# A two-block model layer on one core: query norm moved into the softmax of the cross attention, its heads staggered, and three stretches of work put in another order

## What is computed

```python
# block one
y = concatenate([y_lru, y_ml, y_mo])              # y_mo: 6 heads of block attention
x = x + y @ w_out                                 # "wout": 2048 x 2048
hx = rms_norm(x, xa_norm_g)
hm = rms_norm(mem, mem_norm_g)
x = x + memory_cross_attention(hx, hm, xa_wq, xa_wkv, xa_wo)

def rms_norm(x, g):
    return x * rsqrt(mean(x * x, axis=-1) + eps) * g

def memory_cross_attention(h, mem_n, wq, wkv, wo):   # 4 heads of 128, 256 memory rows
    q = h @ wq
    k, v = split(mem_n @ wkv, 2)
    p = softmax(q @ k.T * 128 ** -0.5)
    return (p @ v) @ wo
```

## Time and profile before

| what | us |
|---|---|
| median of 3 runs | 3553.71 (3549.59 to 3554.19) |
| the profiled execution | 3552.99, its span 3550.9 |
| PE busy | 3402.8 (96%) |
| POOL, ACT, DVE busy | 1386.5, 1069.4, 898.8 |
| granted PE clock, mean of the run | 0.984 of full speed |

### The profile page before, as it was taken

One profiled execution on the slowest core, in us unless ns is written; L12 is line 12 of the kernel. 1 busy time (PEld: TensorE's weight loads), 2 busy tenths in 40 slices (PEclk: granted clock), 3 DMA queues, 4 the chain that ended last, 5 costly groups with the idle time before them and its releaser, 6 DMA issues.

```text
span 3550.9 us, 41542 instructions
## 1 busy us (share of the span) xinstructions
PE 3402.8 (96%) x15611; PEld 2766.7 (78%) x15611; DVE 898.8 (25%) x1498; ACT 1069.4 (30%) x1577; POOL 1386.5 (39%) x601
## 2 busy tenths in 40 slices
PE   6899999999988799999999999999999999999998
PEld 5877878787877477778887877887888887888786
DVE  4275423112124712310022122121111124200213
ACT  5344222223224433422222222223222222222322
POOL 3644333333442333434433333333444444444342
PEclk9999999999999899999999999999999999999998
DMA  6623222232431332233333322332333333333432
GB/s 191 195 61 95 66 77 64 79 83 77 121 109 42 102 87 79 79 85 99 97 83 83 83 78 76 83 83 78 95 96 99 95 98 92 95 99 97 139 95 71
DMA packets 604017, 329.14 MB, mean 93 GB/s; under 512 B 16620, under 2 KB 592372, under 8 KB 602884
## 3 DMA queue, kind: packets, MB, share of 16 engines
q1 hardware_dynamic: 595828, 317.57, 32.0%
q10 hardware_dynamic: 8080, 10.03, 0.9%
HBM read 314.71 MB, written 12.85 MB: 92 GB/s over the span
## 4 chain that ended last, share of the span: by engine, by line
PE 85%; issue 7%; DVE 4%; POOL 2%; ACT 2%; DVEq 0%; ACTq 0%; POOLq 0%
PE proj L614 75%; POOL w_lo L594 2%; PE s L889 2%; PE s L878 1%; PE t L655 1%; PE proj L641 1%; PE s L752 0%; DVE w_st L2531 0%; PE s L1170 0%; DVE ht_lo L1985 0%; DVE xy L2683 0%; DVE xy L2682 0%; DVE xy L2346 0%; PE s L1031 0%; PE s L614 0%
## 5 line engine op out<-in xcount | busy, mean ns | idle before, releaser
L594 POOL TENSOR_TENSOR w_lo<-raw,w_hi 128x1024 fp32r<-128x1024 f32 x572 | 1384.4, 2434 | 2112.5 <-ACT w_hi L1200 2091.7
L614 PE MATMUL proj<-ht_hi,w_hi 128*128 128x512 f32 (+1 forms) x4000 | 1557.2, 389 | 13.3 <-DVE ht_lo L2294 7.0
L614 PE MATMUL proj<-ht_hi,w_lo 128*128 128x512 f32 (+1 forms) x4000 | 1533.2, 383 | 0.0
L614 PE MATMUL proj<-ht_lo,w_hi 128*128 128x512 f32 (+1 forms) x4000 | 1532.6, 383 | 0.0
L614 PEld LDWEIGHTS proj<-ht_hi,w_hi 128*128 128x128 f32 x4000 | 754.4, 189 | 172.5 <-issue 19.7
L614 PEld LDWEIGHTS proj<-ht_lo,w_hi 128*128 128x128 f32 x4000 | 754.7, 189 | 149.9 <-issue 7.0
L614 PEld LDWEIGHTS proj<-ht_hi,w_lo 128*128 128x128 f32 x4000 | 753.9, 188 | 148.8
L1200 ACT ACTIVATE w_hi<-raw 128x1024 fp32r<-128x1024 f32 x570 | 584.2, 1054 | 773.6 <-PE proj L614 732.3
L614 PE MATMUL proj<-yh,w_hi 128*128 128x512 f32 x384 | 150.5, 392 | 3.9 <-DVE yl L2325 2.2
L614 PE MATMUL proj<-yl,w_hi 128*128 128x512 f32 x384 | 150.1, 391 | 0.0
L614 PE MATMUL proj<-yh,w_lo 128*128 128x512 f32 x384 | 150.0, 391 | 0.0
(11 more groups left out here) (473 smaller groups left out, 2321.7 us busy)
## 6 DMA issues: line engine op xcount, KB each, us to landing
raw<-in_w_in_dram SPq DMA_DIRECT2D x404, 512.0 KB, 3.8
raw<-in_w_out_dram SPq DMA_DIRECT2D x64, 512.0 KB, 4.0
raw<-in_xa_wkv_dram SPq DMA_DIRECT2D x16, 512.0 KB, 4.3
raw<-in_w_mem_kv_dram SPq DMA_DIRECT2D x16, 512.0 KB, 4.5
raw<-in_w_br_gla_dram SPq DMA_DIRECT2D x16, 512.0 KB, 3.9
raw<-in_w_br_pool_dram SPq DMA_DIRECT2D x16, 512.0 KB, 3.9
mem_tok<-in_mem_dram SPq DMA_DIRECT2D x4, 1024.0 KB, 8.0
x_tok<-in_x_dram SPq DMA_DIRECT2D x1, 4096.0 KB, 15.3
```

Source lines behind the costliest of these rows:

```text
L594: pool.tensor_tensor(w_lo[:, slot, :], raw[:, slot, :], w_hi[:, slot, :].bitcast(F32), ALU.subtract).then_inc(lo_done, 1)
L614: ins = pe.matmul(dst, w, x[:, kt, c0:c1], start=first and n == 0 and m == 0, stop=last and n == len(kts) - 1 and m == 2)
```

## The change

- **Query norm.** The tiles of x go into the query projection unnormed, scaled by the gain only: ACT's `ht_hi` (`x1_highs`) and DVE's `ht_lo` (`x1_lows`) take `xy` times `xa_norm_g`. The per-token norm `x_r` is one 128x4 column per token tile (`token_sums`, four small matmuls), and goes into the maxima and the exponentials of the softmax as a scale for each row. The tile-wide root, reciprocal and multiplications are gone (1 ACT, 17 DVE instructions), as is the copy to `n_t0`.
- **Heads staggered.** Unit 0 of "xq" runs alone, then unit 1, scores of head 0, unit 2, values of head 0, scores of head 1, unit 3, and so on; head h walks its token tiles from tile h on, and its products go to S[h], so that the next scores need wait only with their last tile.
- **Projection partials.** The first two output tiles of "xwo" are built up kt by kt between the heads (`xwo_part`).
- **Block one's order.** In the first unit of "wout" the last head's values come behind kt 10 in place of kt 7, `out_t` behind kt 14 in place of kt 12, and ACT and DVE make tiles 0 to 14 ahead of the head's work.
- **GLA's last head.** ACT makes `g_kkt` ahead of the gate's tanh.

```diff
+XA_ORDER = [[(h + x) % NT for x in range(NT)] for h in range(XA_HEADS)]
...
+            accumulate(b, 1, proj[0][:], range(8, 11), 0, ht_hi, ht_lo, (0, T), False, False, f, part=True)
             moba_values(MO_HEADS - 1)
-            accumulate(b, 1, proj[0][:], range(8, 13), 0, ht_hi, ht_lo, (0, T), False, False, f, part=True)
+            accumulate(b, 1, proj[0][:], range(11, 15), 3, ht_hi, ht_lo, (0, T), False, False, f, part=True)
             out_t(MO_HEADS - 1, a_o)
-            accumulate(b, 1, proj[0][:], range(13, 16), 5, ht_hi, ht_lo, (0, T), False, True, f)
+            accumulate(b, 1, proj[0][:], range(15, 16), 7, ht_hi, ht_lo, (0, T), False, True, f)
...
+            def token_sums(count, acc, dst):
+                pe.wait_ge(norm_acc, count)
+                for t in range(NT):
+                    ins = pe.matmul(dst[:, 4 * t:4 * t + 4], acc[:, t * P:(t + 1) * P], ones[:, 0:4], start=True, stop=True)
+                ins.then_inc(norm_sum, 1)
...
+            def xa_scores(h):
+                n = A_XA + h
+                taken(qb, h)
+                for t in XA_ORDER[h]:
+                    if t == XA_ORDER[h][-1]:
+                        pe.wait_ge(att_ok, n + 1)
+                    pe.matmul(S[t][:, 0:M], b_q[:, t * P:(t + 1) * P], k1[:, h, :], start=True, stop=True).then_inc(att_s, 1)
...
+                for x, t in enumerate(order):
+                    pe.wait_ge(att_e, n * 4 + x + 1)
+                    if x >= 2:
+                        pe.wait_ge(att_c, n * 4 + x - 1)
+                    transposes(TB[x % 2], [b_l[:, (2 * t + blk) * P:(2 * t + blk + 1) * P] for blk in range(2)]
+                               ).then_inc(att_p, 1)
+                    if x:
+                        product(x - 1)
+                product(NT - 1).then_inc(att_o, 1)
...
+            unit(b, 0, qb, 0, fresh=HT_X1)
+            token_sums(Z_X1 + KT, n_acc, TB[1])
+            unit(b, 2, qb, 1)
+            pe.wait_ge(att_y, MO_HEADS + 1)
+            xa_scores(0)
+            unit(b, 4, qb, 2)
+            xa_values(0)
+            xa_scores(1)
+            unit(b, 6, qb, 3, among=lambda: out_t(A_XA, b_o))
+            pe.wait_ge(yh_ready, YH_XA + 1)
+            xa_values(1)
+            xa_scores(2)
+            out_t(A_XA + 1, b_o)
+            xwo_part(0)
+            pe.wait_ge(yh_ready, YH_XA + 2)
+            xa_values(2)
+            xa_scores(3)
+            out_t(A_XA + 2, b_o)
+            xwo_part(1)
+            pe.wait_ge(yh_ready, YH_XA + 3)
+            xa_values(3)
+            xwo_part(2)
+            out_t(A_XA + 3, b_o)
+            xwo_part(3)
...
             act.wait_ge(att_y, MO_HEADS)
             for k in range(KT):
-                if k == 8:
+                if k == KT - 1:
                     copies(n, a_pt, CAUSAL)
                     ahead(H4["wout"], 0)
-                if k == KT - 1:
                     act.wait_ge(att_y, MO_HEADS + 1)
                 act.activation(ht_hi[:, k, :], xy[:, k, :], ACT.Copy).then_inc(norm_hi, 1)
...
+            ahead(i + H4["wout"], 2)
+            act.wait_ge(bank_free[1], i + Q2["wout"] + 1)
+            x1_highs(range(6))
+            ahead(H4["xq"], 0)
+            squares(xy[:, KT - 1, :], n_sq[:], Z_X1 + KT - 1)
+            x1_highs(range(6, KT))
             nt = {"rstd": n_rstd, "t": [n_t0, n_t1]}
-            root(2)
-            ahead(H4["xq"], 0)
-            highs(4 * H4["xq"], KT)
...
+                    act.wait_ge(att_l, (A_XA + h) * 4 + x + 1)
+                    act.activation(b_l[:, t * M:(t + 1) * M], S[t][:, 0:M], ACT.Exp, bias=b_st[:, t:t + 1],
+                                   scale=x_r[:, t:t + 1], accum_out=b_st[:, 4 + t:5 + t]).then_inc(att_e, 1)
...
+            xa_query(0)
+            ahead(H4["xq"], 2)
+            act.wait_ge(norm_sum, 2)
+            act.activation(x_r, TB[1][:, 0:16].rearrange("p (t c) -> p t c", c=4)[:, :, 0], ACT.Sqrt, scale=1.0 / D,
+                           bias=eps_rms).then_inc(norm_root, 1)
+            xa_query(1)
+            ahead(H4["xq"], 4)
+            xa_exps(0)
+            xa_copies(0)
+            xa_query(2)
+            ahead(H4["xq"], 6)
+            xa_exps(1)
+            xa_high(0)
+            xa_copies(1)
...
+                if last:
+                    gla_kkt(i)
                 unit_in(b, 9)
                 act.activation(g_z[:, 0, :], proj[0][:], ACT.Tanh, scale=0.5).then_inc(gla_act.sem, 1)
                 ahead(b, 10)
-                gla_kkt(i)
+                if not last:
+                    gla_kkt(i)
...
-            lows(xy, HT_Y, None, range(8))
+            lows(xy, HT_Y, None, range(KT - 1))
             out_tokens(MO_HEADS - 1, a_st, a_o)
-            lows(xy, HT_Y, None, range(8, KT - 2))
             moba_y(MO_HEADS - 1)
-            lows(xy, HT_Y, None, range(KT - 2, KT))
+            lows(xy, HT_Y, None, range(KT - 1, KT))
...
+            x1_tile(i + H4["wout"], i, 0)
+            x1_sum(KT - 2)
+            x1_tile(i + H4["wout"], i, 1)
+            x1_lows(range(8))
+            x1_sum(KT - 1)
+            x1_lows(range(8, KT))
+            dve.wait_ge(norm_root, 2)
+            link(dve.reciprocal(x_r, x_r))
...
+                    link(dve.tensor_reduce(b_st[:, t:t + 1], S[t][:, 0:M], AX, MAX, negate=True))
+                    dve.tensor_tensor(b_st[:, t:t + 1], b_st[:, t:t + 1], x_r[:, t:t + 1], MUL).then_inc(att_l, 1)
...
+            xa_logits(0)
+            xa_out(0)
+            xa_logits(1)
+            xa_low(0)
+            xa_out(1)
```

More of the change, by code:

```diff
@@ new lines, in xwo_part @@
+            def xwo_part(kt):
+                for q in range(2):
+                    if kt == 0:
+                        bank_wait(Q2["xwo"], q)
+                    accumulate(wb, 0, proj[q][:], [kt], q + 2 * kt, o_hi, o_lo, (0, T), kt == 0, kt == 3,
+                               (yh_ready, YH_XA), part=kt < 3, done=q == 1)
+            unit(b, 0, qb, 0, fresh=HT_X1)
+            token_sums(Z_X1 + KT, n_acc, TB[1])
+            unit(b, 2, qb, 1)
+            pe.wait_ge(att_y, MO_HEADS + 1)
@@ L981, in xwo @@
+            xa_values(3)
+            xwo_part(2)
+            out_t(A_XA + 3, b_o)
+            xwo_part(3)
+            def xwo(b, qb, first):
+                for q in range(first, 8):
                     bank_wait(qb, q)
                     accumulate(b, q // 2, proj[q % 2][:], range(4), q % 2, o_hi, o_lo, (0, T), True, True,
-                               (yh_ready, YH_XA) if fresh and q == 0 else None, done=q % 2 == 1, step=2)
-            xwo(H4["xwo"], Q2["xwo"], True)
-            xwo(H4["xwo"] + 1, Q2["xwo"] + 4, False)
+                               None, done=q % 2 == 1, step=2)
@@ L987, in _ @@
+            xwo(H4["xwo"], Q2["xwo"], 2)
+            xwo(H4["xwo"] + 1, Q2["xwo"] + 4, 0)
             norm_sums(Z_X2 + 2 * KT, n_acc)
```

153 lines of the change are left out of this document (90 added, 63 removed).

## The result

The changed kernel takes 3534.30 us (median of 5 runs, 3533.81 to 3535.78), the kernel before 3553.71 in the same series (5 runs, 3549.58 to 3556.52). The ratio is 0.9945, its 95% interval 0.9934 to 0.9957. The profiled execution has a span of 3532.0 us against 3550.9, at a granted clock of 0.987 against 0.984. The prediction said 3535.5, and 3528.5 to 3544.

What follows compares the result with a forecast made beforehand. PE was taken as the bound, holding 85% of the chain that ended last. Terms 4.6 + 6.0 + 2.9 + 4.7 = 18.2 us off the profiled 3552.99 gave 3534.8, or 3535.5 from the median; range 3528.5 to 3544.

Steps and rivals of the forecast that it cites:

- Block one: First "wout" unit: reordering lets kt 15 start at 879.2, not 884.67; gain 4.6 us (3.8 to 5.5).
- I take the middle: Block one: 4.6 taken from a gain of 5.5, since a clock fall, left open, would take 1.6.
- The norm: From "wout" to unit 1 of "xq": unit 1 done at 1079.1, not 1085.0; gain 6.0 us (5 to 7).
- a second fall: Unit 0 of "xq": ends at 1067.3, or 1068.6 if the clock falls again; 1067.7 taken.
- The heads: Staggered cross-attention heads: 55.7 us to the last `o_lo`, not 59.5; gain 2.9 us (0.5 to 3.8).
- finds its chain unchanged: Behind the last `o_lo`: DVE sets the pace in "xwo" as before, so only the end of that `o_lo` counts.
- GLA: GLA's last head: no wait for `g_kkt`, states at full clock; gain 4.7 us (4.4 to 4.9).
- The clock falls at each new wait and stays low over the values: Rival, heads: values at half clock cost 6.8 us, not 0.8; gain 12, 3541.5 us; chance 0.13.
- the row on which I set the rule aside: Heads: a 3.12 us idle without a fall, taken over the skill's transpose rule; sum 18, not about 12.
- Norm and heads give nothing: Rival: the last `o_lo` hangs on DVE and ACT; only block one and GLA gain, 9.3, 3544.4 us; chance 0.07.
- the change doesn't do what it says: Rival: the waits come back at the next meeting of engines; within 7 us; chance 0.03.
- slower: Rival: PE's clock stays at 1.2 GHz from 1051 on, through "xq" and "xwo" matmuls; 3578 us; chance 0.03.

Runs made afterwards that it cites:

- shifted: The changed kernel with two memsets of 0.485 us put in on DVE where PE waits for it, ahead of block one; 3539.25 us.
- weights_after_copies: The changed kernel with all 16 high copies on ACT ahead of squares and weight copies, and all 16 low copies first on DVE; 3531.02 us.
- block_one_undone: The changed kernel with block one's old order of kt, values and `out_t` put back on PE, ACT and DVE; 3542.12 us.
- no_fill: The changed kernel with heads still staggered, but all partial products of "xwo" behind the last head; 3539.11 us.
- the control: The changed kernel run again with no edit; 3533.37 us, ratio 0.9936 to the kernel before.
- fills_later: The changed kernel with values earlier in block one, copies ahead of weights in the norm, high copies ahead of exponentials, and "xwo" parts one place later; 3525.71 us.

## Why the prediction was right, step by step

- **Block one**, 4.6 (3.8 to 5.5): measured 5.4 in A, 5.6 when undone. The working gave 5.5, the step "I take the middle" took 0.9 off for a fall that didn't come; in shifted it came, and cost 1.4. No row gave a reason for either case; of the profiled executions with this order only that one lost the clock there, so the 5.5 would have been the better number. Kt 15 was put at 879.2 and stands at 879.50, its idle time at 2.2 and is 2.26.
- **The norm**, 6.0 (5 to 7): measured 5.1. DVE's copies were right: the last ends 17.6 behind the last matmul of "wout", as forecast (1066 less 1048.45). The mis-sized term is the pace of unit 0 behind them. I had one wait of 2 us for kt 7; there are two of 1.8, since tile 6 also comes late behind ACT's weight halves, but kt 7 hangs on its own tile, so the wait at kt 6 costs nothing more. What costs is the clock: I had split the difference between 1067.3 and 1068.6 for a second fall, and it fell behind kt 7's wait. So unit 0 ends 19.8 behind the last matmul of "wout", not 19.3. The first restart kept its clock, which was not foreseen and gained nothing, for PE then waited at kt 6. The token sums take 0.8 and not 0.5; unit 1 takes 11.0 and not 10.9. weights_after_copies shows where the waits come from: 5.0 of B go with them.
- **The heads**, 2.9 (0.5 to 3.8): from scores(0) to the end of the last `o_lo` it takes 55.9 (1130.82 less 1074.91; forecast 55.7). The waits were forecast as 2.4 and 2.4 and are 2.31 and 1.54. The chain in front of them was another than the forecast one: the product behind each maximum makes DVE's step 0.53 and not 0.65, so that DVE no longer sets the pace, but ACT's four exponentials with a scale for each row take 0.54 each, and in the first wait the query's copy (0.60), which the sum left out, stands ahead of them. The two errors nearly cancel in the first wait. No fall came here, so the gain is 3.6, less 0.4 that "xwo" starts later (banks side by side), which "finds its chain unchanged" denied. What the number hid is that it is 4.8 less 1.6. In three other profiled executions with the same code the clock fell behind the first wait; with that fall C is 1.8 to 2.3 us shorter than before, and not 3.2.
- **GLA**, 4.7: 4.64 in the stretch from the norm sums to the head's output product (345.23 to 340.59), 4.84 when undone.
- **The rivals.** "The clock falls at each new wait and stays low over the values" did not happen in the changed kernel, but it does happen: behind 2.32 to 2.34 us in block_one_undone and shifted, and behind 3.71 and 2.93 in no_fill. It costs 1.3 at 2.3 us of waiting (10.47 from the end of one wait to the next in shifted, 9.19 in the control), not the 3.4 I had priced. So the row on which I set the rule aside (3.12 us and no fall) was one sample: behind 3.31 the same products ran at half speed, in both kernels with heads in sequence. The rule of the Trainium skill, "TensorE: Matmul & The Clock Gate", section "Part 4: PE-mode transpose", that transposes don't bring the full clock, doesn't describe this mixed work either: behind 1118.68 in shifted only transposes and small products run, 6 and 8 of them, and at 1122.09 they are back at full length (0.38 for two transposes). No run here has transposes alone. "Norm and heads give nothing", "the change doesn't do what it says" and "slower" are out by the table.
- The terms' errors, +0.8, -0.9, +0.3 and 0, and 0.6 in code that nobody touched, nearly cancel. That the total was only 1.2 off is partly luck; the sizes of the single terms are good to about 1 us.

## What to carry to other kernels

- Read a change by stretches between fixed events, not by the median. Here unedited stretches moved by up to 3.3 us (U) and 1.4 us (C), as much as most single edits are worth: weights_after_copies takes 5.0 us out of its stretch and shows 2.35 in the median.
- Where TensorE waits for a sequence of small copies, look at what stands between them on the copying engine. Two weight copies ahead of tile 6 and one pair of POOL instructions cost 5.0 us with the fall of the clock behind them, four exponentials ahead of one copy, in each of two heads, 2.0.
- Filling a wait pays only where the fill was itself on the path (18 matmuls, 4.1 us of work, gave 1.7 in no_fill); a latency from the last product to the next engine is not shortened by it (fills_later: 0).
